# Panels of the next heads one by one between a head's small products, and the last mixer's groups in another order

## The chip, the cores and the metric

One core of a Trainium2 chip runs the kernel. The metric is the device time of one execution in microseconds (us). TensorE (PE) multiplies, ScalarE (ACT) applies functions, VectorE (DVE) works element by element, GpSimd (POOL) does here only one subtraction, and SyncE (SP) issues the transfers. The five run their own instruction lists in order and meet only at semaphores.

## The reference

The input is 512 tokens of 1024 channels in f32. Two blocks follow each other. The first is a gated attention block (a gMLP branch, an HGRN2 branch with 8 heads of 128, both gated and summed) with a feed-forward part; the second has an mLSTM mixer and an RG-LRU mixer. The diff touches two places of it.

```python
# HGRN2 branch of the first block (8 heads): per head a decayed causal attention, then a norm and a gate
q = silu(zq); log_f = log_sigmoid(zf); k = sigmoid(-zf)
o = hgrn2_chunkwise(q, k, zi, log_f)            # S_t = diag(f_t) S_{t-1} + k_t v_t^T ; o_t = S_t^T q_t
o = rmsnorm(o, norm_g) * silu(zo)
y_a = gmlp_branch(zu, zv, ...) @ w_up_a
y_b = o @ w_up_b
mix = sigmoid(g_a) * y_a + sigmoid(g_b) * y_b   # g_a, g_b are two more column blocks of h @ w_in
x = x + mix @ w_out
...
# RG-LRU mixer (the last mixer): width 1536, 8 blocks of 192
xr, g = split(u @ w_in)
xc = causal_dwconv(xr, conv_w, conv_b)          # 4 taps
r  = sigmoid(blockdiag(xc) @ w_a + b_a); ig = sigmoid(blockdiag(xc) @ w_x + b_x)
a  = exp(-8 * r * softplus(-lam)); bt = sqrt(1 - a*a) * ig * xc
hs = linear_scan(a, bt)                          # h_t = a_t h_{t-1} + bt_t
y  = hs * silu(g);  x = x + y @ w_out
```

## The kernel before

All matrices with activations are kept transposed: channels on the 128 partitions, the 512 tokens along the row. A dense product is made of **panels**: a panel is 128 output channels with all input channels (8 blocks of 128). SP loads a panel into `raw` (line 563), ACT rounds it into `w_hi` (`upper`, line 1108), POOL subtracts to get `w_lo` (line 708, in four pieces), and PE multiplies three times per block, `h_hi*w_hi`, `h_lo*w_hi`, `h_hi*w_lo` (lines 724 to 726, function `dense`). There are four panel buffers and four result banks (0 to 3), each used in turn: panel p may only be rounded when PE has finished panel p - 4, and product t may only be written when ACT or DVE has taken product t - 4 out of its bank. The four other banks (4 to 7) hold small products.

**The heads.** For each of the 8 heads PE makes four panels (forget gate, query, value, output gate; 24 products each) and then small products: `head_scores` has the transposes of v (line 801), eight levels of scores (lines 816 and 822) and the off-diagonal scores (line 834); `head_values` has the products with v (lines 844 to 850) and one sum over channels for the norm (line 853). The loop on PE is

```python
with pe.Fori(0, HH - 1) as i:
    head_in(i + 1, 0)      # two panels of the next head
    head_scores(i)
    head_in(i + 1, 1)      # its two other panels
    head_values(i)
```

and here `head_in(i, half)` stands for two panels at once. After the loop the last head has its scores and its values with no panel between them. Then `ups` begins: groups of eight panels (U_P and following) that make the two gates and the two up-projections; the panel of `w_up_b` (the fourth) waits for the outputs of all heads (`olo_made`).

For the small products ACT and DVE prepare much: ACT makes `lt`, then the exponentials `ee` (line 1184), DVE makes `cum`, the exponents and `qk` (lines 1701 to 1739), DVE takes the scores out under masks (line 1770), ACT copies the off-diagonal scores to `so` (`head_off`, lines 1204 and 1205), squares the values (`head_square`, line 1212) and makes the norm's root (`head_norm`, lines 1216 to 1221). Each of these stands at a fixed place in its engine's list. On ACT the turn of the loop is: a panel's rounding, `head_vT`, `head_soft` of the next head, a rounding, `head_off`, `head_v` of the next head, a rounding, `head_decays` of the next head with `head_square` in it, a rounding, `head_norm`, `head_z`.

**The RG-LRU mixer** runs in 4 groups of 384 channels. A group needs three x panels, a convolution on DVE (`r_conv`: lines 2107 to 2113; its first tap is done by ACT at line 1494), 42 gate products with block-diagonal weights (`r_gates`, lines 1055 to 1057, which wait for the whole convolution), then sigmoids and exponentials on ACT (lines 1511 to 1524), the roots, the scan and the gating on DVE (lines 2128 to 2145). It also has three g panels and four output panels of 18 products (`r_output`), whose results DVE adds to x at line 1823. What PE does in which order is one list for each group (`r_order`): "x" the three x panels, a number a g panel, "a" the gate products, ("o", j) the output panels of group j.

## Time and profile before

| | |
|---|---|
| median of three runs | 1860.75 us (1859.22 to 1861.82) |
| the profiled execution | 1861.52 us |
| its span, from the first instruction to the last | 1859.8 us |
| mean granted TensorE clock | 0.96 |
| PE busy | 1727.7 us, 93% of the span |
| DVE, ACT, POOL busy | 841.0, 841.2 and 853.5 us |
| transfers | 142.88 MB, mean 77 GB/s |

The timeline's rows give the start, the duration, engine, line, operation, names and shapes, how many instructions the row merges, and in brackets the idle time of the engine before it with what ended it. The modelled end of a matmul overlaps the start of the next one, so the distance of two starts tells more than the duration of one. `PEclk` is the share of full TensorE speed that was granted: 1.00 is 2.4 GHz, 0.50 is 1.2 GHz.

The parts of the kernel lie in the trace like this: the heads from about 113 to 449 us, `ups` from 449 us, the feed-forward part, the mLSTM mixer to about 1558 us, the RG-LRU mixer from there to 1834 us.

### The profile page before, as it was taken

To read this page: it belongs to the slowest core of one execution; us is meant where nothing else is said; L and a number is where in the kernel's file an instruction comes from. 1 tells how busy PE (TensorE), PEld (TensorE's weight loads), DVE (VectorE), ACT (ScalarE), POOL (GpSimd) and SP (SyncE) were. 2 spreads that over 40 slices of the span, in tenths; PEclk is the share of its full clock that TensorE was granted. 3 is DMA by queue.
4 is the path that set the end of the run, shared out by engine and by line. 5 is a ranking of instruction groups with operands and counts; after the bars stand their busy time and mean duration, and the time that the engine had idled before them with its cause. 6 is when DMAs were issued, how large, how long until landed. Compare 5 with 4: busy or idle time off the path is not lost.

```text
span 1859.8 us, 21927 instructions
## 1 busy us (share of the span) xinstructions
PE 1727.7 (93%) x7685; PEld 1390.6 (75%) x7685; DVE 841.0 (45%) x1312; ACT 841.2 (45%) x1103; POOL 853.5 (46%) x1094
## 2 busy tenths in 40 slices
PE   3967999997999999999999999999999979988977
PEld 2756788876888888888887777877877757777765
DVE  4254666663111421212135848258167266546643
ACT  3334667565333441323245635445345335653652
POOL 4413233332665655555556535636446425347540
PEclk9978999997999999999999999999999989999988
DMA  4201111211333333333333222322322304123101
GB/s 150 80 23 57 56 48 56 65 45 35 96 91 106 93 100 91 102 91 101 92 90 95 75 57 80 112 58 73 98 68 91 91 13 126 47 85 108 52 30 45
DMA packets 254676, 142.88 MB, mean 77 GB/s; under 512 B 9746, under 2 KB 253203, under 8 KB 254611
## 3 DMA queue, kind: packets, MB, share of 16 engines
q1 hardware_dynamic: 254610, 142.01, 26.3%
q8 instruction: 42, 0.69, 0.1%
q14 instruction: 24, 0.19, 0.0%
HBM read 139.89 MB, written 2.10 MB: 76 GB/s over the span
## 4 chain that ended last, share of the span: by engine, by line
PE 70%; DVE 4%; ACT 3%; issue 2%; ACTq 0%; DVEq 0%
PE bank L724 20%; PE bank L725 20%; PE bank L726 20%; PE bank L1014 2%; PE bank L993 1%; PE bank L978 1%; PE bank L976 1%; PE bank L977 1%; PE bank L1055 1%; PE bank L1057 1%; PE bank L1056 1%; PE bank L822 1%; ACT w_hi L1108 1%; ACT mv L1441 0%; PE bank L834 0%
## 5 line engine op out<-in xcount | busy, mean ns | idle before, releaser
L708 POOL TENSOR_TENSOR w_lo<-raw,w_hi 128x256 fp32r<-128x256 f32 x1056 | 839.6, 827 | 958.7 <-ACT w_hi L1108 958.5
L724 PE MATMUL bank<-h_hi,w_hi 128*128 128x512 f32 x1304 | 527.2, 404 | 26.2 <-POOL w_lo L708 14.1
L1108 ACT ACTIVATE w_hi<-raw 128x1024 fp32r<-128x1024 f32 x264 | 278.3, 1056 | 593.9 <-PE bank L726 568.8
L725 PE MATMUL bank<-h_lo,w_hi 128*128 128x512 f32 x1304 | 513.2, 394 | 0.0
L726 PE MATMUL bank<-h_hi,w_lo 128*128 128x512 f32 x1304 | 512.3, 393 | 0.0
L724 PEld LDWEIGHTS bank<-h_hi,w_hi 128*128 128x128 f32 x1304 | 249.0, 191 | 91.6 <-issue 19.9
L725 PEld LDWEIGHTS bank<-h_lo,w_hi 128*128 128x128 f32 x1304 | 249.0, 191 | 55.5 <-issue 4.5
L726 PEld LDWEIGHTS bank<-h_hi,w_lo 128*128 128x128 f32 x1304 | 248.1, 190 | 53.2
L1823 DVE TENSOR_TENSOR xT<-xT,bank 128x512 f32<-128x512 f32 x104 | 68.5, 684 | 226.8 <-PE bank L726 226.7
L724 PE MATMUL bank<-f_hi,w_hi 128*128 128x512 f32 x256 | 101.3, 396 | 0.0
L725 PE MATMUL bank<-f_lo,w_hi 128*128 128x512 f32 x256 | 101.3, 396 | 0.0
L726 PE MATMUL bank<-f_hi,w_lo 128*128 128x512 f32 x256 | 101.2, 396 | 0.0
L1848 DVE SCALAR_TENSOR_TENSOR fr<-bank,rstd 128x512 f32<-128x512 f32 x32 | 22.1, 692 | 133.7 <-PE bank L726 128.1
L1809 DVE TENSOR_TENSOR gated<-sg,bank 128x512 f32<-128x512 f32 x16 | 11.0, 689 | 120.9 <-PE bank L726 96.6
L724 PE MATMUL bank<-my_hi,w_hi 128*128 128x512 f32 x128 | 52.0, 406 | 10.6 <-DVE my_lo L1920 10.6
L724 PEld LDWEIGHTS bank<-f_hi,w_hi 128*128 128x128 f32 x256 | 48.1, 188 | 11.7
L726 PEld LDWEIGHTS bank<-f_hi,w_lo 128*128 128x128 f32 x256 | 48.1, 188 | 11.6
L725 PEld LDWEIGHTS bank<-f_lo,w_hi 128*128 128x128 f32 x256 | 48.1, 188 | 11.6
L822 PE MATMUL bank<-qk 128*128 128x64 f32 x448 | 56.6, 292 | 0.0
L822 PEld LDWEIGHTS bank<-qk 128*128 128x128 f32 x448 | 56.4, 210 | 0.0
L1184 ACT ACTIVATE ee<-ee 128x512 f32<-128x512 f32 x72 | 42.2, 624 | 24.1 <-DVE ee L1726 24.0
L725 PE MATMUL bank<-my_lo,w_hi 128*128 128x512 f32 x128 | 51.5, 402 | 0.0
(349 smaller groups left out, 2631.2 us busy)
## 6 DMA issues: line engine op xcount, KB each, us to landing
raw<-in_w_ff SPq DMA_DIRECT2D x64, 512.0 KB, 4.0
raw<-in_w_in SPq DMA_DIRECT2D x56, 512.0 KB, 3.7
raw<-in_m_w_in SPq DMA_DIRECT2D x48, 512.0 KB, 3.9
raw<-in_r_w_in SPq DMA_DIRECT2D x24, 512.0 KB, 3.9
raw<-in_m_w_out SPq DMA_DIRECT2D x16, 512.0 KB, 3.3
raw<-in_r_w_out SPq DMA_DIRECT2D x16, 384.0 KB, 3.0
raw<-in_w_up_b SPq DMA_DIRECT2D x8, 512.0 KB, 4.1
raw<-in_w_out SPq DMA_DIRECT2D x8, 512.0 KB, 4.0
```

The source lines that it names most:

```text
L708: ins = pool.tensor_tensor(w_lo[:, s, part], raw[:, s, part], w_hi[:, s, part].bitcast(F32), ALU.subtract)
L724: pe.matmul(dst, wh, hi[:, k, :], start=(k == 0), stop=False)
L725: pe.matmul(dst, wh, lo[:, k, :], start=False, stop=False)
L726: mm = pe.matmul(dst, wl, hi[:, k, :], start=False, stop=(k == kt - 1))
L822: mm = pe.matmul(dst, qk[:, m - 1, c], right, start=True, stop=True, skip_group_check=True)
L976: pe.matmul(dst, xm_hi[:, k, c], wh, start=(k == 0), stop=False, skip_group_check=True)
L977: pe.matmul(dst, xm_hi[:, k, c], wl, start=False, stop=False, skip_group_check=True)
L1014: mm = pe.matmul(bank[t % RING][:, n * P:S], mv[:, n, d * P:(d + 1) * P], st[:, place_st[n]:place_st[n] + w], start=(n == 0), stop=(n == N ...
L1108: act.activation(w_hi[:, p % RING, :], raw[:, p % RING, :], ACT.Copy).then_inc(hi_ready[p % RING], 1)
L1184: act.activation(ee[:, l % 3, :], ee[:, l % 3, :], ACT.Exp).then_inc(decay_made, 1)
L1823: dve.tensor_tensor(xT[:, j, :], xT[:, j, :], bank[t % RING][:], ALU.add).then_inc(taken[t % RING], 1)
L1848: dve.scalar_tensor_tensor(fr[:, e % 2, :], bank[(F_T + e) % RING][:], 0.0, rstd[:], ALU.max, ALU.mult).then_inc(taken[(F_T + e) % RING], 1)
```

## The change

Four things change.

1. `head_in(i, n)` is one panel. On PE the order in a turn is now levels, panel 2 of the next head, off-diagonal scores, panel 3, values, panel 0 of the head after that, the norm's sum, panel 1. `head_scores` is split into `head_levels` and `head_off`, `head_values` into `head_values` and `head_sum`. The last turn before the last head has the first two panels of `ups` where the others have panels 0 and 1.
2. In the first group of `ups` the fifth panel's work comes before the fourth's (`UP_AT`, `up_at`), on SP, PE, ACT and DVE.
3. ACT's list in a head's turn: `head_off` now lies inside `head_decays`, after its second exponential, `head_square` before its eighth; the roundings of panels are at other places and one panel further ahead. DVE no longer waits for the off-diagonal scores before `head_prepare`, but before `qk` of level 7.
4. The RG-LRU mixer: group 0 has its gate products before its second g panel; groups 1 and 2 have both g panels and the gate products before the output panels of the group before. The first tap goes from ACT to DVE. The roundings, adds and g products are placed anew on ACT and DVE. The gate weights come in 8 transfers of whole rows for each group instead of 16.

In the order of the instructions, on ACT in a head's turn (`so` is the copy of the off-diagonal scores, `hf` that of v, `kk` the key, `ee` the exponentials). Before:

```order
L1175 ACTIVATE lt<-lt 128x512
L519 REGISTER_ALU
L1108 ACTIVATE w_hi<-raw 128x1024
L1204 ACTIVATE so<-bank 128x512
L1205 ACTIVATE so<-bank 128x256
L1206 ISA
L1207 REGISTER_ALU
L1190 ACTIVATE hf<-bank 128x512
L1108 ACTIVATE w_hi<-raw 128x1024
L1179 ACT_TABLE_LOAD
L1179 ACTIVATE kk<-kk 128x512
```

And now, at the same place:

```order
L1205 ACTIVATE lt<-lt 128x512
L1222 ACTIVATE hf<-bank 128x512
L1138 ACTIVATE w_hi<-raw 128x1024
L1209 ACT_TABLE_LOAD
L1209 ACTIVATE kk<-kk 128x512
L1215 REGISTER_ALU
L1216 ACTIVATE ee<-ee 128x512
L1215 REGISTER_ALU
L1216 ACTIVATE ee<-ee 128x512
L1236 ACTIVATE so<-bank 128x512
L1237 ACTIVATE so<-bank 128x256
```

The two copies to `so` stood before `hf` and now stand behind the second `ee`; the rounding between `lt` and `so` is gone from here.

On DVE in group 1 of the mixer (`rt`, `ri` the roots and inputs of the scan, `xT` the sum with the output panels' products, `rh` the scan's result, `rg` a g product). Before, all eight adds stood between the convolution and the first root:

```order
L2102 TENSOR_TENSOR rc_lo<-rc,rc_hi 128x512
L1823 TENSOR_TENSOR xT<-xT,bank 128x512 x8
L2128 SCALAR_TENSOR_TENSOR rt<-hf,rt 128x512
L2130 TENSOR_TENSOR ri<-ri,rc 128x512
L2128 SCALAR_TENSOR_TENSOR rt<-hf,rt 128x512
```

Now:

```order
L2143 TENSOR_TENSOR rc_lo<-rc,rc_hi 128x512
L2165 TENSOR_TENSOR rg<-bank,rstd 128x512
L1864 TENSOR_TENSOR xT<-xT,bank 128x512 x2
L2171 SCALAR_TENSOR_TENSOR rt<-hf,rt 128x512
L2173 TENSOR_TENSOR ri<-ri,rc 128x512
L1864 TENSOR_TENSOR xT<-xT,bank 128x512 x2
L2171 SCALAR_TENSOR_TENSOR rt<-hf,rt 128x512
```

A second g product has come in ahead, and the adds lie in pairs between the roots.

The diff, cut to its core (the sync engine's and the vector engine's parts of `ups`, which follow `up_at`, are left out):

```diff
+UP_AT = [0, 1, 2, 4, 3, 5, 6, 7]
+def up_at(i, n):
+    return UP_AT[n] if isinstance(i, int) and i == 0 else n
...
     if i == 0:
-        return ["x", 0, 1, "a", 2]
+        return ["x", 0, "a", 1, 2]
     if i < RG - 1:
-        return ["x", 0, ("o", i - 1), "a", 1, 2]
+        return ["x", 0, 1, "a", ("o", i - 1), 2]
...
-                    sp.dma_start(gw[:, z, 0, :], w[0:P, 0:P]).then_inc(gw_loaded, 16)
-                    sp.dma_start(gw[0:64, z, 1, :], w[P:192, 0:P]).then_inc(gw_loaded, 16)
-                    (and six more)
+                    sp.dma_start(rows[:, 0:192], w[0:P, :]).then_inc(gw_loaded, 16)
+                    sp.dma_start(rows[0:64, 2 * P:2 * P + 192], w[P:192, :]).then_inc(gw_loaded, 16)
+                    (and two more)
...
# PE
-            head_in(0, 0)
-            head_in(0, 1)
-            with pe.Fori(0, HH - 1) as i:
-                head_in(i + 1, 0)
-                head_scores(i)
-                head_in(i + 1, 1)
-                head_values(i)
-            head_scores(HH - 1)
+            for n in range(H_N):
+                head_in(0, n)
+            head_in(1, 0)
+            head_in(1, 1)
+            with pe.Fori(0, HH - 2) as i:
+                head_levels(i)
+                head_in(i + 1, 2)
+                head_off(i)
+                head_in(i + 1, 3)
+                head_values(i)
+                head_in(i + 2, 0)
+                head_sum(i)
+                head_in(i + 2, 1)
+            head_levels(HH - 2)
+            head_in(HH - 1, 2)
+            head_off(HH - 2)
+            head_in(HH - 1, 3)
+            head_values(HH - 2)
+            up(0, 0)
+            head_sum(HH - 2)
+            up(0, 1)
+            head_levels(HH - 1)
+            head_off(HH - 1)
             head_values(HH - 1)
+            head_sum(HH - 1)
+            for n in (2, 4, 3, 5, 6, 7):
+                up(0, n)
...
# ACT
                 for l in range(len(LEVELS)):
-                    if l == 3 and before is not None:
+                    if l == 2 and before is not None:
+                        head_off(before)
+                    if l == 7 and before is not None:
                         head_square(before)
...
             def heads(i):
-                upper(H_P + 7, i, H_N)
+                upper(H_P + 9, i, H_N)
                 head_vT(i)
                 head_soft(i + 1)
-                upper(H_P + 8, i, H_N)
-                head_off(i)
                 head_v(i + 1)
-                upper(H_P + 9, i, H_N)
+                upper(H_P + 10, i, H_N)
                 head_decays(i + 1, i)
-                upper(H_P + 10, i, H_N)
+                upper(H_P + 11, i, H_N)
                 head_norm(i)
                 head_z(i + 1)
+                upper(H_P + 12, i, H_N)
...
+            def r_follow(i, e):
+                if 0 < i < RG - 1:
+                    follow(R_OP[i - 1] + e)
             def r_gates(i):
                 (the six sigmoids)
+                r_follow(i, 0)
                 (tanh, exponential and square of each of three tiles)
+                r_follow(i, 1)
                 (the three square roots)
+                r_follow(i, 2)
...
# DVE
                     tile_full(dve, R_XP[i] + c)
                     dve.tensor_tensor(xr[:, c, PAD:], bank[(R_XT[i] + c) % RING][:], rstd[:], ALU.mult)\
                        .then_inc(taken[(R_XT[i] + c) % RING], 1)
-                    dve.wait_ge(tap_made, f + 1)
+                    tile_taken(dve, R_XT[i] + c)
+                    link(dve.tensor_scalar(rc[:, c, :], xr[:, c, 1:1 + S], r_tap(0, f), col("r_conv_b_2", f),
+                                           ALU.mult, ALU.add))
...
             for i in range(RG):
                 r_conv(i)
+                if i:
+                    r_gate(i, 1)
+                out = 0 < i < RG - 1
                 for c in range(RT):
+                    if out:
+                        r_add(i - 1, 2 * c)
+                        r_add(i - 1, 2 * c + 1)
                     r_root(i, c)
```

## Rows read from the trace of the kernel before

**Rows 1.** The page: busy time (part 1), and the rounding of a panel (part 5).

```profile
PE 1727.7 (93%) x7685; PEld 1390.6 (75%) x7685; DVE 841.0 (45%) x1312; ACT 841.2 (45%) x1103; POOL 853.5 (46%) x1094
...
L1108 ACT ACTIVATE w_hi<-raw 128x1024 fp32r<-128x1024 f32 x264 | 278.3, 1056 | 593.9 <-PE bank L726 568.8
```

**Rows 2.** Timeline of PE, one turn of the head loop.

```profile
241.52 0.60 PE L801 MATMUL bank<-ident,hf 128*128 128x128 f32 x4
242.84 6.36 PE L822 MATMUL bank<-qk 128*128 128x64 f32 x56
250.31 2.92 PE L834 MATMUL bank<-qk 128*128 128x128 f32 x8 [1.10 <-DVE sd L1770]
...
267.32 1.12 PE L853 MATMUL bank<-sq,ones 128*128 128x512 f32 x2 [0.69 <-ACT sq L1212]
...
279.22 0.49 PE L801 MATMUL bank<-ident,hf 128*128 128x128 f32 x3
```

**Rows 3.** Windows: a:b, us, busy time (instructions) by engine, PEclk, DMA, GB/s.

```profile
205.90:212.70 6.80, 5.70 (x52) 5.56 (x51) 4.14 (x8) 6.73 (x10) 2.79 (x4) 1.00 0.10 28
212.70:216.10 3.40, 3.40 (x10) 2.86 (x11) 0.52 (x1) 1.89 (x4) 2.04 (x3) 0.50 0.33 98
```

**Rows 4.** Timeline of PE, the last head.

```profile
417.60 1.12 PE L853 MATMUL bank<-sq,ones 128*128 128x512 f32 x2 [0.69 <-ACT sq L1212]
426.26 1.12 PE L801 MATMUL bank<-ident,hf 128*128 128x128 f32 x4 [7.53 <-ACT rstd L1216]
...
441.59 2.93 PE L834 MATMUL bank<-qk 128*128 128x128 f32 x8 [0.67 <-DVE sd L1770]
445.61 0.88 PE L844 MATMUL bank<-so,vT 128*128 128x384 f32 x2 [1.09 <-ACTq L1208]
...
449.28 0.79 PE L724 MATMUL bank<-h_hi,w_hi 128*128 128x512 f32 x1
```

**Rows 5.** Timeline of ACT, the same turn as in rows 2.

```profile
241.90 0.63 ACT L1221 ACTIVATE o_hi<-hf 128x512 f32 x1 [1.73 <-DVE hf L1784]
...
245.28 0.59 ACT L1200 ACTIVATE vT<-bank 128x512 f32<-128x512 f32 x1
...
253.27 0.60 ACT L1204 ACTIVATE so<-bank 128x512 f32<-128x512 f32 x1 [1.59 <-PE bank L834]
...
259.04 0.60 ACT L1190 ACTIVATE hf<-bank 128x512 f32<-128x512 f32 x1 [4.89 <-PE bank L726]
...
262.43 1.66 ACT L1184 ACTIVATE ee<-ee 128x512 f32<-128x512 f32 x3
...
273.94 1.28 ACT L1216 ACT_TABLE_LOAD   x1
```

**Rows 6.** Timeline of PE, waits in the start of the heads and in the mixer.

```profile
152.40 0.80 PE L724 MATMUL bank<-h_hi,w_hi 128*128 128x512 f32 x1 [8.31 <-POOL w_lo L708]
...
1702.07 0.77 PE L724 MATMUL bank<-y_hi,w_hi 128*128 128x512 f32 x1 [5.64 <-issue]
...
1771.47 0.76 PE L1055 MATMUL bank<-rc_hi,gw_hi 128*128 128x512 f32 x1 [6.31 <-issue]
```

**Rows 7.** Windows: the gate products of group 0, and from their end to group 3's.

```profile
1585.50:1595.00 9.50, 9.50 (x43) 7.84 (x42) 0.69 (x1) 6.20 (x8) 2.82 (x4) 1.00 0.25 82
1595.00:1783.20 188.20, 169.29 (x703) 137.59 (x702) 111.70 (x130) 102.89 (x134) 96.38 (x104) 0.94 0.24 71
```

**Rows 8.** Timeline of DVE in the mixer: group 0, and the convolution of group 1.

```profile
1569.76 0.75 DVE L2113 SCALAR_TENSOR_TENSOR rc<-xr,cols,rc 128x512 f32<-128x512 f32 x1
...
1619.39 0.68 DVE L2107 TENSOR_TENSOR xr<-bank,rstd 128x512 f32<-128x512 f32 x1
1620.95 1.54 DVE L2111 SCALAR_TENSOR_TENSOR rc<-xr,cols,rc 128x512 f32<-128x512 f32 x2 [0.88 <-ACT rc L1494]
...
1632.27 1.21 DVE L2113 SCALAR_TENSOR_TENSOR rc<-xr,cols,rc 128x512 f32<-128x512 f32 x1
...
1636.43 0.69 DVE L2102 TENSOR_TENSOR rc_lo<-rc,rc_hi 128x512 fp32r<-128x512 f32 x1 [1.22 <-ACT rc_hi L1501]
```

More of the change, by code:

```diff
@@ L788, in _, with head_in, head_levels @@
                 mm.then_inc(mixed, 1)
-            def head_in(i, half):
-                for e in (0, 1):
-                    dense(H_P + 2 * half + e, H_T + 2 * half + e, i, H_N)
-            def head_scores(i):
+            def head_in(i, n):
+                dense(H_P + n, H_T + n, i, H_N)
+            def head_levels(i):
                 def free(b, n):
@@ L862, in _ @@
-            head_scores(HH - 1)
-            head_values(HH - 1)
-            def ups(i, need_a=None, need_b=None):
-                for e in range(2):
-                    dense(U_P + 4 * e, U_T + 4 * e, i, U_N)
-                    pe.wait_ge(ya_made, GG)
-                    dense(U_P + 4 * e + 1, U_T + 4 * e + 1, i, U_N, hi=ya_hi, lo=ya_lo, kt=4)
-                    dense(U_P + 4 * e + 2, U_T + 4 * e + 2, i, U_N)
-                    pe.wait_ge(olo_made, HH)
-                    dense(U_P + 4 * e + 3, U_T + 4 * e + 3, i, U_N, hi=o_hi, lo=o_lo)
@@ L874, in _, with up @@
-            with pe.Fori(0, DT // 2) as i:
-                ups(i)
+            def up(i, n):
+                if n % 4 == 1:
+                    pe.wait_ge(ya_made, GG)
+                if n % 4 == 3:
+                    pe.wait_ge(olo_made, HH)
+                hi, lo = {1: (ya_hi, ya_lo), 3: (o_hi, o_lo)}.get(n % 4, (h_hi, h_lo))
+                at = up_at(i, n)
+                dense(U_P + at, U_T + at, i, U_N, hi=hi, lo=lo, kt=4 if n % 4 == 1 else 8)
+            for n in range(H_N):
+                head_in(0, n)
@@ L876, in _ @@
+            up(0, 0)
[3 more added lines that the diff above has]
+            head_off(HH - 1)
+            head_values(HH - 1)
+            head_sum(HH - 1)
+            for n in (2, 4, 3, 5, 6, 7):
+                up(0, n)
+            with pe.Fori(0, DT // 2 - 1) as i:
+                for n in range(U_N):
+                    up(i + 1, n)
             for j in range(DT):
@@ L1818, in _ @@
             dve.sem_inc(mix_made, 1)
-            steps.loop(DT // 2, 0, ups)
+            ups(0)
+            steps.loop(DT // 2 - 1, 0, ups, 1)
             def add_x(j, p, t, i=0, per_p=0, per_t=0):
@@ L2171, in _ @@
                 r_scan(i, 2)
[L2172 removed]
+                r_lower_y(i, 1)
+                if i < RG - 1:
+                    r_gate(i, 2)
                 r_y(i, 2)
```

114 lines of the change are left out of this document (57 added, 57 removed).

## The prediction

> **What bounds the kernel now.** The page's busy times come first: TensorE is busy 93% of the span, no other engine half of it [rows 1]. So only what TensorE loses can be won: idle time, and time at the lower clock. I then read its timeline for gaps, the windows for the clock at those gaps, and last the lists of ScalarE and VectorE, which decide whether another wait comes in the place of one that goes.
>
> In the head loop a turn is the distance from line 801 to line 801: 279.22 - 241.52 = 37.70 us, and there are seven [rows 2]. It has two gaps: 1.10 us before the off-diagonal scores (VectorE is still taking the levels out under their masks) and 0.69 before the norm's sum (ScalarE is squaring). There is a third loss. In the turn before, the clock was full over the levels and the gap behind them, 205.9 to 212.7, with TensorE busy 5.70 of 6.80 us, and then 0.50 for 3.40 us [rows 3]. The off-diagonal products and the start of the next panel fall into that: 3.4 us of work at half speed is a loss of 1.7. After the loop the last head has no panels between its products: from 417.60 to 449.28, 31.7 us, with a wait of 7.53 for the norm's root, levels at half clock from 426.26 to 440.9, and waits of 0.67 and 1.09 [rows 4].
>
> In the mixer TensorE waits three times for more than 5 us: before the output panels of groups 0 and 1 and before the last gate products (one of the three is 5.64, one 6.31) [rows 6]. The releaser is given as "issue", since the wait is for bank tiles that VectorE had not yet taken. The code says why: VectorE begins the convolution of a group only when it has finished the group before (1619.39 in group 1, that is 24.4 us after the gate products ended at 1595.0), and the convolution ends at about 1637.0 [rows 7, 8]. From 1595.0 to 1783.2 TensorE is busy 169.3 of 188.2 us, so 18.9 are idle, at a granted clock of 0.94: 0.06 x 188.2 = 11.3 us of lost clock, on stretches of 22.6 us at half, about 5 us of which are themselves idle. The loss in work is then about 9 us, and 28 in all.
>
> **The head turns.** Nothing is added to TensorE's work; panels move. Behind the levels a panel now starts at once, and the off-diagonal scores come one panel later (24 products; 43 take 9.5 us [rows 7], with the next one's start 5.4 us), when the masks are long done: the 1.10 is gone. Behind the values comes a panel of 5.4 before the sum: the square (0.6 us on ScalarE) fits in, the 0.69 is gone. The low clock came after a stretch of thin products and a gap; without the gap I take it that it stays full, -1.7. Together 3.5.
>
> What is late next? ScalarE, in three places.
> (a) `so` must be there before the values. The copies now stand behind the second `ee`. In rows 5 the copy of v starts at 259.04 and the second `ee` is over 4.5 us later; two more copies (the first 0.60) make 5.6 after the panel's end. TensorE has in that time the off-diagonal scores (1.3 at full clock) and a panel, 6.7. It fits by 1 us.
> (b) The square is behind the seventh `ee`. Exponentials run at VectorE's pace and the last one ended at 272.9 (a rounding, 1.06 [rows 1], before 273.94), so the seventh at about 270: 11 us after the copy of v. TensorE comes to the sum 1.3 + 5.4 + 2.4 (values: 445.61 to 449.28 less wait and sum [rows 4]) + 5.4 = 14.5 us after the same point. It fits by 2.
> (c) The loop over the norm: sum, root (the first table load at 273.94), then `o_hi` 5.6 us later, output gate, and now two roundings of panels instead of one before `vT`, whose copy ends 4.0 + 1.0 us after `o_hi` starts [rows 5]. `vT` frees bank 7, which the sixth of the eight levels needs first, 5.0 us after the turn's start (1.3 and four times a seventh of 6.36 [rows 2]). With the root starting 1.2 us after the sum and the new turn 6.5 us after it, `o_hi` is at +0.3 of the new turn and `vT` done at +5.3. A stall of 0.3 us comes in.
> Two more joins of thin and dense work: 0.15 each. So 3.5 - 0.6 = 2.9 us a turn, 7 turns: **-20 us**. Bounds: if the clock still falls and the stall doubles, 7 x 1.0 = -7; if (c) costs nothing, 7 x 3.5 = -25.
> Panels themselves are not short: the one that ScalarE rounds last in its turn (after the output gate, +4 us in the new turn) is used at +22.
>
> **The last head.** Between the sum of the head before and its levels now lies a short panel (2.7 us) that was in `ups`, and another (5.4) before the sum. The wait of 7.53 becomes: root's first half done 3.2 us after the sum starts, TensorE there after 3.7. Nothing. `vT` is late by 2.1 (its place in the list is behind `o_hi` and the output gate). So: sum 1.0, levels 7.7 at full clock, stall 2.1, masks 1.1, off-diagonal 2.9 (as in rows 4, at half clock), wait 1.1, values and sum with its wait 3.7: 19.6 instead of 31.7. **-12 us**; bounds -8 (levels again half at half clock) and -15 (no stall).
> The fourth panel of `ups` needs `olo_made` of the last head, some 7.5 us after its sum; two panels of 5.4 now stand before it. No wait, as before.
>
> **The mixer.** Work on TensorE stays the same. In group 0 the gate products come one panel earlier, at 1585.5 - 5.4 = 1580.1, and wait for the convolution, which was only just over when they began at 1585.5. The rounding of its last tile no longer stands behind a silu with its table load (as line 1216's, 1.28 and 0.6 [rows 5]), and the taps on VectorE save part of the 0.88 waits [rows 8]; I put the start at 1582.1, a new wait of 2 (bounds 0 and 4). From its end at 1591.6 group 0's chain goes as before, with one g product and its silu more in it, and ends 2.4 us earlier, at 1617, and the convolution of group 1 takes 15.9 instead of 17.7 (three waits of 0.88 against three taps at the price of line 2113, 0.75 to 1.21, and the 1.22 before the last `rc_lo` is gone): it ends at 1633. TensorE has seven panels after the gate products, 1591.6 + 38.1 = 1629.7: a wait of 3.3, and 2.5 of lost clock. In groups 1 and 2 TensorE has 49 us between its gate products (four output panels of 4.1, six panels of 5.4), and VectorE and ScalarE need 4 us more than in group 0 because the tanh now stands behind a rounding that waits for the first output panel; the convolution is through 48 to 50 us after the gate products. A wait of about 1 each. New losses 2 + 3.3 + 2.5 + 2 = 9.8 against 28: **-18 us**. At the end the adds of group 3 are the same. Bounds: -5 (see rival 2) and -25 (only the first wait is left).
> The gate weights in 8 transfers instead of 16 save SyncE about 4 us of issuing, off the path: SyncE now issues them before the output panels' loads, behind the split on VectorE, and those loads still come 7 us or more before the rounding needs them except in group 2, where it is about even.
>
> On the tap, the rows give line 2113 as 0.75 us when GpSimd rests and 1.21 while it splits a panel [rows 8]: a slowdown of half. The Trainium skill (SBUF — State Buffer, "Who interferes with whom") says that a tensor_scalar can take the port pair shared with GpSimd, and that the one that comes second blocks fully. By that rule a tap may wait for a whole piece of the split, and GpSimd for the tap; by the rows it is slower by half a microsecond at most.
>
> **The sum.** 20 + 12 + 18 = 50 from the profiled execution's 1861.5 gives 1811.5. The median is 0.8 below that execution, within the scatter of the runs; I take 1811.
>
> **Rivals.**
> 1. The clock still falls once in each turn. For it: the thin levels are unchanged, 7.7 us. Against it: in rows 3 the stretch before the fall has TensorE idle for 1.1, and that idle time goes. Time: 7 x 1.7 less 1 for stalls it covers, +11: 1822.
> 2. The mixer's chain is the bound in every group. For it: three roundings in ScalarE's list that wait for TensorE's output panels, each holding back tanh, root or gating. Against it: the adds no longer stand before the roots. Then groups 1 and 2 wait 5 us each with 2.5 of lost clock, +12.5: 1823.5. With rival 1: 1835.
> 3. The taps block on GpSimd's pieces: nine taps on the path by 0.70 (GpSimd's four pieces take 2.79 [rows 3]) are 6.3: 1817. The rule named above stands behind this one.
> 4. The turn doesn't get shorter, because ScalarE's list with its waits on VectorE closes the loop at 37: only the last head and the mixer gain, 1831. Against it: its wait of 4.89 for the panel [rows 5] is slack.
> 5. Slower. The ring of four panels runs dry in the head loop: the rounding that now comes last in ScalarE's turn, behind the norm and the output gate, reaches GpSimd after TensorE wants the panel. The price is the wait at the start of the heads, 8.31 us [rows 6], and again half clock, 1.7: a turn of 34.8 + 10.0 = 44.8, 7 x 7.1 = +50 against before, so 1861.5 + 50 - 12 - 18 = 1881. It decides from the point where that rounding is more than 15 us late; nothing in rows 5 is.
>
> **Chances.** Forecast 0.48; rival 1 0.20; rival 2 0.13, with rival 1 0.04; rival 3 0.06; rival 4 0.04; rival 5 0.03; no change within 0.2% 0.02. The forecast's own range is 1802 to 1819; for 8 in 10 I take in rivals 1 to 3 and let the far ends of the bounds go: 1801 to 1831. A change under 0.2% (3.7 us) could not be told from none here. Faster 0.95, same 0.02, slower 0.03.
>
> **What would show it.** Right: distance of the transposes in the head loop 34.8 us, no wait before the off-diagonal scores nor before the sum, a wait of about 0.3 inside the levels; granted clock full from 170 to 405; first dense product behind the last head's sum near 426 with two panels of `ups` done; gate products of group 3 starting near 1723 (1771.5 less 32 in the heads and 16 to 17 of the mixer). Wrong: clock 0.5 behind the levels in each turn (rival 1), waits of 5 us before the gate products of groups 2 and 3 (rival 2), `w_lo` as releaser in the head loop (rival 5).

## The result, and the profile after

| | before | after |
|---|---|---|
| median (range) | 1861.1 us (1859.22 to 1861.82) | 1820.3 us (1817.84 to 1821.09) |
| ratio | | 0.978, interval [0.9765, 0.9794] |
| span of the profiled execution | 1859.8 us | 1818.3 us |
| mean granted TensorE clock | 0.96 | 0.973 |

The kernel is 41 us faster; 50 were forecast, so 1811 was 9 us too low. I split the difference at one instruction, TensorE's first product of the last mixer that waits for a low part of its input: it starts at 1558.54 before and at 1526.30 after. Up to there 32.2 us are won (forecast: 20 + 12), behind it 9.3 (forecast: 18). The whole error of the sum lies in the mixer; those in the heads cancel, as shown below.

The page after, the rows that answer to [rows 1] (busy time and share of each engine):

```profile
PE 1706.8 (94%) x7685; PEld 1373.9 (76%) x7685; DVE 859.6 (47%) x1324; ACT 824.7 (45%) x1084; POOL 860.1 (47%) x1094
...
L1138 ACT ACTIVATE w_hi<-raw 128x1024 fp32r<-128x1024 f32 x264 | 277.5, 1056 | 614.3 <-PE bank L735 578.4
```

TensorE has as many products as before, 7685, and is busy 21 us less: products at half clock count twice as long.

**A turn of the head loop** after, TensorE's timeline without its dense rows (compare [rows 2]):

```profile
267.68 0.60 PE L809 MATMUL bank<-ident,hf 128*128 128x128 f32 x4
...
272.96 2.89 PE L830 MATMUL bank<-qk 128*128 128x64 f32 x24 [0.27 <-ACT vT L1232]
281.22 1.47 PE L843 MATMUL bank<-qk 128*128 128x128 f32 x8
...
295.68 1.02 PE L864 MATMUL bank<-sq,ones 128*128 128x512 f32 x2
302.02 0.60 PE L809 MATMUL bank<-ident,hf 128*128 128x128 f32 x4
```

The turn is 34.34 us. The off-diagonal scores (line 843) take 1.47 instead of 2.92 and wait for nothing, nor does the sum (line 864). One wait of 0.27 is left, for the copy of v. The windows of the whole loop and of the last head (us, busy time and count by engine, PEclk, DMA share, GB/s; compare [rows 3]):

```profile
170.00:402.00 232.00, 230.77 (x1264) 196.66 (x1263) 162.14 (x401) 163.65 (x221) 75.78 (x104) 1.00 0.19 57
402.00:424.00 22.00, 17.69 (x92) 15.27 (x91) 6.40 (x11) 6.87 (x10) 3.45 (x5) 0.69 0.17 49
```

**The last head** after (compare [rows 4]):

```profile
398.64 1.02 PE L864 MATMUL bank<-sq,ones 128*128 128x512 f32 x2
...
409.30 4.86 PE L830 MATMUL bank<-qk 128*128 128x64 f32 x24 [2.00 <-ACT vT L1232]
414.82 2.93 PE L843 MATMUL bank<-qk 128*128 128x128 f32 x8 [0.67 <-DVE sd L1808]
418.84 1.62 PE L852 MATMUL bank<-so,vT 128*128 128x384 f32 x2 [1.09 <-ACTq L1240]
...
424.22 1.10 PE L864 MATMUL bank<-sq,ones 128*128 128x512 f32 x2 [0.78 <-ACT sq L1244]
424.75 0.79 PE L733 MATMUL bank<-h_hi,w_hi 128*128 128x512 f32 x1
```

The wait of 7.53 is gone, and the dense work goes on at 424.75. But the window above has the clock at 0.69: the second half of the levels takes 4.86 us, the off-diagonal scores 2.93 and the values up to the sum about 5.4, nearly all at the lower level.

**The mixer** after: the first gate product of each of the four groups, from TensorE's timeline (compare [rows 6]):

```profile
1549.86 0.68 PE L1085 MATMUL bank<-rc_hi,gw_hi 128*128 128x512 f32 x1 [3.59 <-issue]
1603.89 0.47 PE L1085 MATMUL bank<-rc_hi,gw_hi 128*128 128x512 f32 x1 [4.55 <-issue]
1668.27 0.47 PE L1085 MATMUL bank<-rc_hi,gw_hi 128*128 128x512 f32 x1 [3.49 <-issue]
1731.45 0.47 PE L1085 MATMUL bank<-rc_hi,gw_hi 128*128 128x512 f32 x1 [2.30 <-issue]
```

And the windows from the end of one group's gate products to the end of the next one's (compare [rows 7]):

```profile
1526.30:1561.10 34.80, 30.37 (x123) 23.96 (x124) 17.47 (x22) 16.97 (x20) 13.68 (x17) 0.95 0.38 105
1561.10:1615.10 54.00, 49.45 (x211) 40.44 (x210) 36.03 (x42) 30.95 (x41) 27.02 (x28) 0.97 0.27 79
1615.10:1679.50 64.40, 60.91 (x259) 49.48 (x259) 43.05 (x49) 33.38 (x43) 37.77 (x40) 0.97 0.28 83
1679.50:1741.10 61.60, 59.30 (x260) 48.33 (x259) 43.25 (x49) 33.39 (x43) 38.15 (x40) 1.00 0.23 71
```

The waits for the banks before the output panels are gone. But every group now waits before its gate products: 3.6 + 4.6 + 3.5 + 2.3 = 13.9 us idle. In the first three the 42 gate products take 11.2 to 11.3 us instead of the 9.65 of the last, 4.8 lost in all at the lower clock.

### The profile page after: what moved, and what is told of

The parts are those of the page before. It is cut to its first block, busy times and chain, and to the rows that moved or that the text cites. A ratio compares the mean times of both kernels' runs of the same rounds, so it can differ in the third digit from the quotient of the medians.

```text
span 1818.3 us, 21831 instructions
## 1 busy us (share of the span) xinstructions
PE 1706.8 (94%) x7685; PEld 1373.9 (76%) x7685; DVE 859.6 (47%) x1324; ACT 824.7 (45%) x1084; POOL 860.1 (47%) x1094
## 4 chain that ended last, share of the span: by engine, by line
PE 81%; DVE 8%; ACT 6%; issue 4%; POOL 1%; ACTq 0%; DVEq 0%; POOLq 0%
PE bank L733 23%; PE bank L735 23%; PE bank L734 23%; PE bank L1044 2%; PE bank L830 2%; ACT w_hi L1138 2%; DVE ee L1762 1%; DVE qk L1776 1%; PE bank L1023 1%; PE bank L1085 1%; PE bank L1008 1%; PE bank L1006 1%; PE bank L1007 1%; DVE qk L1777 1%; PE bank L1086 1%
```

## Why the mixer waits: group 1 read closely

ScalarE after, from the last sigmoid of group 1 on (TensorE's gate products ended at 1615.15):

```profile
1615.35 0.69 ACT L1548 ACTIVATE ri<-bank,cols 128x512 f32<-128x512 f32 x1 [0.68 <-PE bank L1087]
1619.63 1.06 ACT L1138 ACTIVATE w_hi<-raw 128x1024 fp32r<-128x1024 f32 x1 [3.60 <-PE bank L735]
1620.60 0.71 ACT L1554 ACTIVATE rt<-rr,cols 128x512 f32<-128x512 f32 x1
...
1658.41 1.06 ACT L1138 ACTIVATE w_hi<-raw 128x1024 fp32r<-128x1024 f32 x1 [9.14 <-DMA raw<-in_r_w_out]
```

ScalarE has all it needs for the tanh at 1616.0, but a rounding stands first in its list, and that waits until TensorE has finished the first output panel: 3.60 us, then 1.06 for the rounding itself. VectorE waits with it:

```profile
1619.55 1.28 DVE L1864 TENSOR_TENSOR xT<-xT,bank 128x512 f32<-128x512 f32 x2 [15.16 <-PE bank L735]
1624.03 0.69 DVE L2171 SCALAR_TENSOR_TENSOR rt<-hf,rt 128x512 f32<-128x512 f32 x1 [3.19 <-ACT hf L1559]
```

From the end of the gate products to the start of the next convolution it is 26.2 us in group 0, and 35.6 (to 1650.72) in group 1. The last row of ScalarE above is the third delay. A panel's load comes late, so the rounding of the convolution's result, which stands behind it, comes late too. SyncE's list says why the load is late: the eight gate-weight transfers start only when VectorE has split the old weights, and the loads stand behind them.

```profile
1649.68 0.34 SPq L650 DMA_DIRECT2D gw<-in_r_w_a  x1
...
1653.78 0.59 SPq L654 DMA_DIRECT2D gw<-in_r_w_x  x1
1654.48 1.45 SPq L570 DMA_DIRECT2D raw<-in_r_w_out  x3
```

## The experiments

Each ran beside the kernel before on the same chip (1860.6 to 1861.3 us there). "After" is 1820.3.

**1. The heads alone.** `ups` and the heads as after; the mixer's orders, its tap and its transfers as before. The first lines of that edit are

```diff
     if i == 0:
-        return ["x", 0, "a", 1, 2]
+        return ["x", 0, 1, "a", 2]
     if i < RG - 1:
-        return ["x", 0, 1, "a", ("o", i - 1), 2]
+        return ["x", 0, ("o", i - 1), "a", 1, 2]
...
```

> The heads and the first group of the up-projections as in the changed kernel, the mixer as before. The traces of the two kernels put 32.2 us of the gain before the mixer's first x panel (1558.54 against 1526.30). Theory (the parts are independent, the mixer brought about 9): 1829, that is 32 under the kernel before. Rival (the mixer's part needs the state that the heads leave, or brought more and the heads less): above 1833 or below 1826.

Measured 1827.3 us, ratio 0.9819 [0.9803, 0.9835]. From the first waited product to the end of the last gate products it is 224.6 us, as before (224.7). So the theory holds: the heads' gain doesn't need the mixer's part. By the medians 34 us come from the heads and 7 from the mixer. In the traces the mixer's stage is 9.8 shorter after; the difference lies in the scatter ahead of it (the stage starts at 1524.78 here and at 1526.30 after, with the same instructions before it) and behind it.

**2. The off-diagonal scores behind the levels again.**

```diff
     head_levels(i)
-    head_in(i + 1, 2)
     head_off(i)
+    head_in(i + 1, 2)
     head_in(i + 1, 3)
```

> The changed kernel, but with the off-diagonal scores again directly behind the levels in the seven head turns, and the two panels behind them. Theory (the gap of 1.1 us behind the levels is what brings the lower clock): a turn is longer by 1.1 of idle time and 1.7 of half clock, the clock falls in each turn, 7 x 2.8 = 20 us: 1840. Rival (the clock follows the thin levels and only happens to be full now): 7 x 1.1 = 8, the clock stays full: 1828.

Measured 1860.9 us, ratio 0.9996 [0.9986, 1.0006]: the whole gain is gone, and both numbers missed. The mixer keeps its gain (its stage is 215.4 us), so the heads alone are some 10 us longer than before: the stage starts at 1568.6. TensorE's timeline and windows of one turn, which is 40.8 us:

```profile
209.72 5.16 PE L830 MATMUL bank<-qk 128*128 128x64 f32 x24 [0.99 <-ACT vT L1232]
215.71 2.93 PE L843 MATMUL bank<-qk 128*128 128x128 f32 x8 [0.84 <-DVE sd L1808]
```

```profile
203.70:210.00 6.30, 5.31 (x48) 5.16 (x46) 4.45 (x8) 5.30 (x8) 1.77 (x3) 1.00 0.25 75
210.00:220.20 10.20, 9.36 (x37) 8.43 (x37) 5.72 (x18) 4.38 (x6) 3.76 (x6) 0.50 0.36 103
```

Two things changed together. The gap before the off-diagonal scores is back, and the copy of v is late: 0.99 instead of 0.27, inside the levels. The clock fell there and stayed low for 10.2 us. So this run says that the gain hangs on the order, not which of the two stalls takes it. The 10.2 us are those of five turns; the first has 3.4 and the last 6.8.

**3. The same, with the copy of v early.** In ScalarE's list the rounding that stood before `head_vT` goes behind `head_soft`.

```diff
-                upper(H_P + 9, i, H_N)
                 head_vT(i)
                 head_soft(i + 1)
+                upper(H_P + 9, i, H_N)
```

> The run with the off-diagonal scores directly behind the levels, and ScalarE copies v out of its bank before it rounds the panel that it rounded first. Theory (the gain was lost because the copy of v came late, the levels waited about 1 us and the clock fell inside them): the wait inside the levels goes, the clock stays full, and a turn costs only the gap of about 1 us before the off-diagonal scores: turn 35.2, time 1828. Rival (the gap before the off-diagonal scores lowers the clock by itself): the clock falls behind the levels for about 3.4 us, turn 36.9, time 1840.

Measured 1837.8 us, ratio 0.9875 [0.986, 0.989]: the rival, 1840. The turn (201.22 to 238.60) is 37.4 us and has one stall, of 1.11, before the off-diagonal scores. The windows up to it and behind it:

```profile
201.20:210.28 9.08, 7.92 (x69) 7.63 (x68) 5.81 (x11) 8.02 (x10) 2.78 (x4) 1.00 0.21 61
210.28:213.70 3.42, 3.42 (x10) 2.94 (x11) 2.52 (x3) 1.67 (x3) 1.66 (x2) 0.52 0.45 130
```

The clock falls to half for 3.42 us behind the gap, as in [rows 3]. The turn is 3.0 longer than one of 34.34. From start to start, 1.1 of it lies in the levels with the gap (7.74 for 6.65, which had the stall of 0.27 in it), 1.2 in the off-diagonal scores (2.28 for 1.12) and 0.7 in the two panels behind them. By the clock alone it is 0.48 x 3.42 = 1.6.

But this holds for five of the seven turns. In the sixth the gap of 1.11 is there, and the clock stays full behind it; in the seventh a gap of 0.94 does nothing either.

```profile
359.60:366.00 6.40, 6.39 (x30) 5.45 (x31) 5.22 (x12) 1.68 (x3) 3.74 (x4) 1.00 0.24 72
```

The sixth turn is 35.65 us. So the gap in place of the stall of 0.27 costs 1.3, and the clock about 1.7 more where it falls. Putting the gap back confirms the forecast's first term and its price, but not that the fall must come. Before, it came in all seven turns; why not here in two is open. Between this run and the one before lie 23 us; they are what the late copy of v costs in this order.

**4. The first rounding of the mixer behind the tanh block** (ScalarE, `r_gates`).

```diff
-                r_follow(i, 0)
                 for c in range(RT):
                     (tanh, exponential, square)
+                r_follow(i, 0)
                 r_follow(i, 1)
```

> The changed kernel, but in mixer groups 1 and 2 the rounding that waits for the first output panel comes behind the tanh, exponential and square on ScalarE instead of before them. Theory A (this rounding in front of the tanh holds the chain of a group by its 4.4 us): the waits before the gate products of groups 2 and 3 (3.5 with half clock behind it, and 2.3) vanish, -7: 1813. Theory B (VectorE's adds, which wait for the output panels and stand before the roots, hold it as well, to the third output panel at 12.4 us after the gate products): the roots end 1 us earlier in each group, -2 to -3: 1818.

Measured 1818.1 us, ratio 0.9775 [0.9758, 0.9791]. The interval overlaps that of after, so the trace has to decide: the stage is 212.9 us instead of 214.8, which is B. The waits before the gate products are 3.6, 5.5, 2.6 and 1.6, and the clock stayed full in group 2. The distance from a group's gate products to the next convolution fell by 0.7 alone, to 34.9: VectorE's first adds, which wait for the same output panel, still stood before the first root. (The wait before group 1, which the edit doesn't touch, is 1.0 longer than after: that much is scatter.)

**5. The output panels' loads before the gate weights**, on SyncE alone.

```diff
-                for what in r_order(i):
+                turns = r_order(i)
+                if 0 < i < RG - 1:
+                    at = turns.index("a")
+                    turns[at], turns[at + 1] = turns[at + 1], turns[at]
+                for what in turns:
```

> The changed kernel, but in mixer groups 1 and 2 SyncE issues the loads of the output panels before the gate weights' transfers, not behind them. In the changed kernel ScalarE waits 8.2 and 9.1 us for these loads in front of a rounding, VectorE then 0.4 and 1.4 for the rounded tile, and GpSimd splits four panels in one go beside the convolution. Theory C (the late loads cost the convolution): both waits vanish and the convolution is a microsecond shorter, -2 to -4: 1817. Rival (the waits are slack): 1820, unchanged.

Measured 1816.8 us, ratio 0.976 [0.9744, 0.9777]. The stage is 211.9, 2.9 less, and ScalarE's waits of 8 to 9 us for these loads are gone. The waits before the gate products are 3.8, 4.3, 2.3 and 2.3, that is 1.2 less in all; the other 1.6 or so is the clock, which stayed full in the gate products of group 2 (9.65 us). The distance from the gate products to the next convolution is unchanged, 35.6; the convolutions of groups 1 and 2 are 16.25 us instead of 16.5 and 17.45. By the medians it is a gain of 3.5, about as wide as the scatter of one kernel; the trace carries the verdict.

**6. The short chain.** Experiment 5, and on ScalarE all three roundings behind the square roots; VectorE begins with the first root:

```diff
-                for c in range(RT):
-                    if out:
-                        r_add(i - 1, 2 * c)
-                        r_add(i - 1, 2 * c + 1)
-                    r_root(i, c)
+                r_root(i, 0)
+                adds(0)
+                r_root(i, 1)
+                r_root(i, 2)
+                adds(2)
...
                 r_scan(i, 0)
-                if out:
-                    r_add(i - 1, 6)
-                    r_add(i - 1, 7)
+                adds(4)
+                if out:
+                    r_scan(i, 1)
+                adds(6)
```

Here `adds(e)` makes the adds e and e + 1 in groups 1 and 2.

> The run with the output panels' loads first, and in groups 1 and 2 ScalarE makes tanh, exp, square and the roots' square roots before it rounds anything, and VectorE makes the first root before it adds. Theory (the chain from one group's gate products to the next convolution is what TensorE waits for, and roundings that wait for output panels lie in it): the waits before the gate products of groups 2 and 3 go from 2.3 to 0.3 or less, with the stage at 208 us; time 1812. Rival (VectorE's own work beside GpSimd is the chain, the order doesn't matter): waits unchanged, 1816 to 1817.

Measured 1812.2 us, ratio 0.9738 [0.9725, 0.9751]: the theory. No wait is left before the gate products of groups 2 and 3, and their clock is full. The stage is 207.3 us. The wait of 4.3 before those of group 1 is still there, since group 0 has no output panels beside its chain.

**7. Group 0 in its old order**, the silus and g products with it.

```diff
     if i == 0:
-        return ["x", 0, "a", 1, 2]
+        return ["x", 0, 1, "a", 2]
```

> Only group 0 in the order of before: both g panels, then the gate products, and the second silu before the sigmoids. Theory (the chain is the bound): the wait of 3.6 before the gate products of group 0 goes and the wait of 4.6 before those of group 1 grows to about 9, since group 0's gate products end at the same time and its chain is as long; time 1820 to 1821. Rival (the new order of group 0 costs its wait and its low clock, 3.6 + 1.7): 1815.

Measured 1817.9 us, ratio 0.9771 [0.9757, 0.9784], between the two; its interval overlaps that of after. The trace gives both a part. The waits are 0, 8.12, 3.43 and 2.30, in all 13.85 against 13.93 after: idle time only moved, as the theory said.

```profile
1601.02 0.76 PE L1085 MATMUL bank<-rc_hi,gw_hi 128*128 128x512 f32 x1 [8.12 <-issue]
```

But from its first gate product to the product behind its last, group 0 is back at 9.6 us, and so is group 2; group 1 takes 12.2. That is 2.6 us of lost clock in all for 4.8. A wait of 3.43 before the products of group 2 cost nothing here, and one of 3.49 after cost 1.6.

**8. The first tap back on ScalarE.**

```diff
+                    tile_taken(act, R_XT[i] + c)
+                    act.activation(rc[:, c, :], xr[:, c, 1:1 + S], ACT.Identity, scale=r_tap(0, i * RT + c),
+                                   bias=col("r_conv_b_2", i * RT + c)).then_inc(tap_made, 1)
...
-                    tile_taken(dve, R_XT[i] + c)
-                    link(dve.tensor_scalar(rc[:, c, :], xr[:, c, 1:1 + S], r_tap(0, f), col("r_conv_b_2", f),
-                                           ALU.mult, ALU.add))
+                    dve.wait_ge(tap_made, f + 1)
```

> Only the first tap back on ScalarE, with VectorE's wait for it. Theory (the convolution is in the chain; a tap on VectorE costs 0.55 to 0.95, the hand-over to ScalarE and back 0.88 and more): 1.0 to 1.5 us more in each of the four groups, 1825. Rival (a tap on VectorE blocks with GpSimd's pieces and costs as much as the hand-over): 1820.

Measured 1826.2 us, ratio 0.981 [0.9797, 0.9824]: the theory's number, by another way than it said. Here are VectorE's second and third taps in the convolution of group 1, for each of its three tiles of 128 channels, and then ScalarE's rows around the middle one:

```profile
1589.18 1.84 DVE L2156 SCALAR_TENSOR_TENSOR rc<-xr,cols,rc 128x512 f32<-128x512 f32 x2 [0.89 <-ACT rc L1531]
...
1596.33 2.47 DVE L2156 SCALAR_TENSOR_TENSOR rc<-xr,cols,rc 128x512 f32<-128x512 f32 x2 [3.91 <-ACT rc L1531]
...
1602.55 1.80 DVE L2156 SCALAR_TENSOR_TENSOR rc<-xr,cols,rc 128x512 f32<-128x512 f32 x2 [0.88 <-ACT rc L1531]
```

```profile
1594.53 1.06 ACT L1139 ACTIVATE w_hi<-raw 128x1024 fp32r<-128x1024 f32 x1 [5.38 <-DMA raw<-in_r_w_out]
1595.50 0.80 ACT L1531 ACTIVATE rc<-xr,cols 128x512 f32<-128x512 f32 x1
```

The plain hand-over costs 0.88, and 3.91 where the tap stands behind a rounding that waits for a late load. The waits before the gate products are 3.5, 7.4, 6.7 and 2.1 = 19.7, that is 5.8 more than after, all in the two groups that follow a late load. So the tap on VectorE also keeps the convolution clear of ScalarE's roundings.

**9. `ups` in its old order.**

```diff
-UP_AT = [0, 1, 2, 4, 3, 5, 6, 7]
+UP_AT = [0, 1, 2, 3, 4, 5, 6, 7]
```

> Only the first group of the gates and up-projections in its old order, so the panel that needs all heads' outputs comes after one panel of 5.4 instead of two. Theory (the last head's output, ready at 430.92 in the changed kernel, would be late by 0.8): a wait of about 0.8 before that panel, time 1821. Rival (the wait is larger, since the low part of the output is late by the whole chain of 7.5 behind the sum, less 5.4, and the clock falls): a wait of 2.1 and 1 to 2 of clock, 1824.

Measured 1823.7 us, ratio 0.9801 [0.9786, 0.9816]. It does not test the step. TensorE's list has its order written out by itself (`for n in (2, 4, 3, 5, 6, 7)`), so that only the slots changed: TensorE still took the panel on h first, out of a slot loaded and freed one later, and waited 1.36 for the bank that ScalarE had to take (`sg`, line 1295). The median is near the rival's 1824, but the profiled execution is the fastest of the four, 0.8 us longer than that of after, and the intervals overlap. Neither theory nor rival is decided. What the old order costs with TensorE's list changed too was not tried.

**10. The copy of v early, alone.** The edit of experiment 3 on the kernel after.

> Only ScalarE's copy of v moved ahead of the rounding that stood before it at the start of a turn. Theory (that rounding of about 1 us makes the wait of 0.25 to 0.27 inside the levels): the wait goes in seven turns, turn 34.0 instead of 34.3, 1.9 in all, 1818.4. Rival (the copy is held by the norm's chain, not by the rounding): wait and time stay, 1820.3.

Measured 1820.5 us, ratio 0.9779 [0.9766, 0.9793]: no change. The rival's time, not its reason. The wait inside the levels does shrink, to 0.2 and less, and the first turns are 33.88 us. But from the fourth on they are 34.6 (with a wait of 0.14 before the values), and the stall in the last head is 2.57 instead of 2.00. The rounding's new place moves GpSimd's piece onto VectorE's exponents:

```profile
L1762 DVE TENSOR_TENSOR ee<-cum 128x256 f32<-128x256 f32 x36 | 21.5, 598 | 0.0
L1761 DVE TENSOR_TENSOR ee<-cum 128x256 f32<-128x256 f32 x36 | 20.6, 573 | 1.4
```

This is VectorE by lines, 200 to 400 us: busy time, then mean ns of one. In the kernel after the means are 510 and 424.

**11. Low parts behind the convolution.** Experiment 6, and on VectorE (groups 0 to 2, taken out of their own group):

```diff
                 if i:
                     r_gate(i, 1)
+                    for c in range(RT):
+                        r_lower_y(i - 1, c)
```

> The run with the short chain, and VectorE makes the three low parts of y of groups 0 to 2 behind the next group's convolution instead of before it (1.23, 1.04 and 1.23 us in group 0). Theory (VectorE's list from gate products to convolution sets the wait before the gate products of group 1, 4.3 there): that wait falls by 3.4 to about 0.9 and the clock there stays nearer full; time 1807 to 1809. Rival (the wait is set by ScalarE's functions, VectorE only follows): 1811 to 1812.

Measured 1808.1 us, ratio 0.9711 [0.9698, 0.9725]: the theory's time, and the fastest kernel of this study, 12 us under the kernel after and 53 under that before. The waits before the gate products are 4.10, 2.40, 0 and 0, and the stage is 203.5 us. The windows of groups 1 to 3, bounded as in those of the kernel after:

```profile
1561.50:1611.80 50.30, 47.90 (x212) 39.34 (x211) 37.20 (x42) 30.94 (x41) 28.58 (x28) 1.00 0.25 76
1611.80:1670.80 59.00, 59.00 (x260) 48.38 (x259) 43.24 (x49) 33.62 (x43) 39.67 (x40) 1.00 0.31 92
1670.80:1729.80 59.00, 59.00 (x259) 48.40 (x258) 43.33 (x49) 33.62 (x43) 39.83 (x40) 1.00 0.24 74
```

Groups 2 and 3 have not a gap in 59.0 us. In group 1 the wait fell by 1.9 and not 3.4: 3.5 us of low parts left VectorE's list, but the convolution begins only 2.0 earlier (1585.43 against 1587.41) and is 0.4 longer. The clock came back in its gate products all the same (9.63 us for 11.26), and the two make 3.5 of the 3.8 us.

**12. Experiment 11, and the copy of v before two roundings.**

```diff
             def heads(i):
-                upper(H_P + 9, i, H_N)
                 head_vT(i)
                 head_soft(i + 1)
+                upper(H_P + 8, i, H_N)
+                upper(H_P + 9, i, H_N)
...
                 head_z(i + 1)
-                upper(H_P + 12, i, H_N)
...
             head_vT(last)
+            upper(U_P + 4)
```

> The run before (low parts behind the convolution), and in the heads ScalarE copies v first and rounds two panels behind the next head's functions, so also in the last head one rounding less stands before the copy of v. Theory (both waits for v shrink): 1.9 in the seven turns and 0.9 of the 2.0 in the last head, 2.8 less than the run before, about 1804. Rival (the panels rounded later reach TensorE late): w_lo appears as releaser in the head loop and the time rises above the run before.

Measured 1815.1 us, ratio 0.9754 [0.9741, 0.9768]: 7 us slower than experiment 11. The rival's direction, with another mechanism: `w_lo` never appears as releaser. TensorE waits before the values, for the copy of the off-diagonal scores, 1.53 to 1.57 in five turns and 1.18 in another (8.9 in all), and a turn is 35.7 us. In the last head the stall for v fell to 1.63, with a new wait of 0.50 ahead of its transposes. VectorE's exponents of the next head, and GpSimd's block that lies on them:

```profile
322.62 0.96 DVE L1765 TENSOR_TENSOR ee<-cum 128x256 f32<-128x256 f32 x1
...
325.27 0.95 DVE L1764 TENSOR_TENSOR ee<-cum 128x256 f32<-128x256 f32 x1
326.14 0.41 DVE L1765 TENSOR_TENSOR ee<-cum 128x256 f32<-128x256 f32 x1
```

```profile
315.89 10.04 POOL L721 TENSOR_TENSOR w_lo<-raw,w_hi 128x256 fp32r<-128x256 f32 x12 [11.51 <-ACT w_hi L1142]
```

Each exponent is 0.96 until GpSimd's three panels end at 325.9, and 0.41 at once behind. The copies wait for the second exponential, and so for these. The stall before the values did not touch the clock, unlike the gap of experiment 3:

```profile
318.00:328.00 10.00, 8.46 (x40) 6.71 (x39) 9.73 (x19) 6.11 (x9) 7.93 (x11) 1.00 0.42 121
```

## Why the prediction was right, and where it was not

**The head turns: right, a little low.** Forecast 34.8 us, measured 34.2 in the mean of the six full turns (165.46 to 370.71), against 37.65 before; no wait before the off-diagonal scores nor the sum; none to 0.27 inside the levels for a forecast of 0.3; the clock full over the whole loop. With the seventh turn (up to its sum 25.6 us before, 27.9 after with one more panel of 5.5) it is 20.6 + 3.2 = 23.8 for a forecast of 20. The two joins of thin and dense work, put at 0.15 each, are part of what was not there. That the clock would come back with the gap was only taken; experiment 3 shows that the gap can bring the fall, in five turns of seven. Step (a), "It fits by 1 us", is the next bound: experiments 10 and 12 cross it, with waits of 0.14 and 1.5, by slowing VectorE before the second exponential. Step (b) held, with no wait anywhere.

**The last head: the mechanism right, the size 3 us too large.** From one sum to the dense work behind the next it is 424.75 - 398.64 = 26.1 us; without the short panel (3.2) 22.9, for 19.6 forecast and 31.7 before. So -8.8 and not -12, near the bound of -8. The term that failed is "levels 7.7 at full clock": they took 9.9, since the clock fell behind the stall of 2.00 (forecast 2.1), and the "values and sum" of 3.7, read at full clock in [rows 4], took 5.9. The two errors in the heads cancel, and that is luck: 32.6 of gain, with 0.6 won ahead of the first turn and 0.9 lost behind, for 32.

**The mixer: mis-sized, 9.3 instead of 18.** The step that failed is the one on the waits before the gate products.

| group | wait forecast | measured | gate products forecast | measured |
|---|---|---|---|---|
| 0 | 2 | 3.6 | full clock | 11.2, 1.6 lost |
| 1 | 3.3 | 4.6 | 2.5 lost | 11.3, 1.6 lost |
| 2 | about 1 | 3.5 | full clock | 11.25, 1.6 lost |
| 3 | about 1 | 2.3 | full clock | 9.65 |

New losses of 13.9 + 4.8 = 18.7 stand against 9.8 forecast, about the 9 that are missing.

Group 0's longer wait is no loss of its own. Its gate products start 23.6 us behind the stage's start, as forecast (1582.1 less 1558.5); the wait is longer because TensorE gets there sooner. Before, 3.4 us at half clock lay in the panels ahead of them, and after they don't; in experiment 9 they are back, and the wait is 2.18. The windows up to the gate products before (with one panel more), and up to the wait after; the last field but two is the clock:

```profile
1558.54:1585.46 26.92, 26.09 (x105) 20.41 (x106) 15.32 (x19) 14.46 (x17) 13.21 (x17) 0.94 0.44 119
1526.30:1546.30 20.00, 19.13 (x80) 14.82 (x80) 14.07 (x17) 8.75 (x10) 10.88 (x13) 1.00 0.57 156
```

The 1.7 us won there, which the forecast doesn't have, are offset by about 1 inside the stage that no row places, and by 0.6 lost behind it. In group 1 the convolution is through 42.7 us after the gate products of group 0, for 41.4 forecast.

In groups 2 and 3 it is through 53.0 and 51.8 us after, for "48 to 50". The forecast has VectorE and ScalarE need "4 us more than in group 0" up to the convolution; they needed 9.3 more (35.6 for 26.2). I had seen that the tanh stands behind a rounding and put 4 us for it, but not that VectorE's first adds hold the first root by the same output panel (experiments 4 and 6). And I had called the gate-weight transfers "off the path", "except in group 2, where it is about even". They were not: the loads behind them were 8 to 9 us late and held the roundings that the convolution needs (experiment 5, 2.9 us; experiment 8, where the tap shares that list). Experiment 6 removes all three, and the waits before groups 2 and 3 go.

**The range.** 1820.3 lies just outside the forecast's own range, 1802 to 1819, and inside 1801 to 1831, which was made wide enough for rivals 1 to 3. Of the signs named, the dense work behind the last head (424.75 for "near 426") came true, and the last gate products (1731.45 for "near 1723") did not.

**The rivals.** Rival 1 (the clock falls anyway): no, 1.00 in every turn of the loop. Rival 2 (the mixer's chain binds in every group) is what happened, at less than its price: waits of 3.5 and 2.3 for 5 and 5 and 1.6 of clock, lost in one of the two groups, for 2.5. It gave 1823.5, the forecast 1811; the result, 1820.3, is nearer to the rival. Rival 3 (the taps block): a tap takes 0.55 us alone and 0.94 to 0.95 beside GpSimd, in eight of twelve, so the price is 3.1 and not 6.3. Whether it waits or is slowed, its own rows don't say. The rows of other shapes in the trace after say more: beside GpSimd a VectorE instruction on two tensors in SBUF takes 0.54 longer whether it is 128x256 (0.42 to 0.96), 128x512 (0.68 to 1.22) or 128x896 (1.08 to 1.63), and copies of 128x2 and 128x4 go from 0.16 to 0.69 and from 0.17 to 0.51. An addition that doesn't grow with the size looks like a wait and not like sharing by a factor. By the rule of the Trainium skill (SBUF — State Buffer, "Who interferes with whom") the later one would wait in full; these rows speak for it, though what a tap adds, 0.40, is less than a whole piece of 0.70. Rival 4 (ScalarE closes the loop at 37): no; but VectorE's exponents close it at 35.7 once GpSimd lies on them. Rival 5 (ring dry): no, and not in experiment 12 either, where two roundings are later still.

## What to carry to other kernels

When a long wait goes from an in-order engine's list, go through that list again with every instruction that waits for TensorE, and ask what stands behind it. Here a rounding, a pair of adds and a row of transfers together kept two waits alive. The first two stood in the way from one group's gate products to the next convolution (35.6 us long, and 32.1 without them in experiment 6), and the third made the convolution itself longer. Put what closes the loop to TensorE first, and what only feeds later work (the low parts, the roundings of panels that are used 15 us on) behind it; moves of this kind gave 12 us more. And count a slowed neighbour: moving one rounding moves GpSimd's piece, and that can double the price of what VectorE does on the path.

## What was not expected of the hardware

- Neither a stall's length nor its place tells alone what the clock does behind it. Inside the thin products 0.27 and 0.17 us left it full, and 0.99 in experiment 2 brought half clock; directly behind them 1.11 brought it in five turns of experiment 3 and left it full in the sixth; 1.53 to 1.57 behind a dense panel (experiment 12) left it at 1.00 in five turns.
- Before the gate products there were 41 waits in the twelve kernels with the changed mixer. Of 14 waits of 1.6 to 2.6 us one cost clock in the products behind it (1.5 us); of 12 of 3.1 to 3.6 all but one did (1.4 to 2.5); of 15 of 3.8 to 8.1 all did (1.3 to 2.9). The price grows little with the wait: the three longest, 6.7 to 8.1, cost 2.2 to 2.6.
- Two stalls in a turn, 0.99 and 0.84, came with 10.2 us at half clock between and behind them, and the single gap of 1.11 with 3.42: 23 us over seven turns for 0.7 us more of idle time in each. The stall of 0.99 was never tried alone.
- GpSimd beside VectorE adds nearly the same 0.54 us to an instruction on two tensors in SBUF whatever its size, so small ones suffer most: an exponent more than doubles.
- A transfer order worth nothing by issue time (half as many transfers, 0.3 to 0.6 us each) cost 2.9 us by what was queued behind it.
